# Low parts of the down-projection weights made by VectorE instead of GpSimd in the two feed-forward layers of a hybrid decoder step

## What is computed

```python
def conv_ffn(h, prev, w_up, conv_w, conv_b, w_down):
    u = h @ w_up                                     # 1024 -> 2 * 2816
    t = u.shape[1]
    xp = jnp.concatenate([prev.astype(u.dtype), u], axis=1)
    c = conv_b
    for j in range(CONV_W):
        c = c + conv_w[j] * xp[:, j:j + t]
    val, gate = c[..., :D_FF], c[..., D_FF:]
    return (jax.nn.silu(gate) * val) @ w_down, xp[:, t:]
```

## Time and profile before

| | |
|---|---|
| time, median of 3 runs | 3090.78 us (3090.75 to 3100.58) |
| span of the profiled execution, first to last instruction | 3083.6 us |
| TensorE busy | 2933.5 us (95%) |
| VectorE busy | 1911.6 us (62%) |
| ScalarE busy | 968.2 us (31%) |
| GpSimd busy | 371.0 us (12%) |
| DMA | 174.37 MB, mean 57 GB/s |

### The profile page before, as it was taken

How to read it: one execution, slowest core, us unless ns; L and a number is a source line. 1 busy time by engine, 2 the same in 40 slices (tenths; PEclk the granted TensorE clock), 3 DMA queues, 4 the chain that set the end, 5 groups by cost and what they waited for, 6 DMA issues and landing times. The chain is left out here.

```text
span 3083.6 us, 54554 instructions
## 1 busy us (share of the span) xinstructions
PE 2933.5 (95%) x19232; PEld 2750.7 (89%) x19232; DVE 1911.6 (62%) x3783; ACT 968.2 (31%) x1739; POOL 371.0 (12%) x396
## 2 busy tenths in 40 slices
PE   8979889999998999999999988989989999999998
PEld 5646679998996899999999988989989999999998
DVE  3436667777775565666666666882246566666665
ACT  3433345555554322222222223222122222222221
POOL 1003300000000000000000018660000000000000
PEclk9988999999998999999999999999999999999999
DMA  3010013222221021111111114343111111111111
GB/s 111 28 23 1 35 46 81 73 75 70 75 74 47 27 62 42 41 48 47 48 41 54 35 45 138 87 110 119 49 58 49 42 44 51 41 47 46 49 35 69
DMA packets 262263, 174.37 MB, mean 57 GB/s; under 512 B 77977, under 2 KB 247658, under 8 KB 261818
## 3 DMA queue, kind: packets, MB, share of 16 engines
q1 hardware_dynamic: 261882, 171.85, 19.2%
q10 hardware_dynamic: 192, 0.13, 0.0%
HBM read 149.49 MB, written 22.29 MB: 56 GB/s over the span
## 5 line engine op out<-in xcount | busy, mean ns | idle before, releaser
L1641 PE MATMUL f_up<-h_hi,f_wu_hi 128*128 128x352 f32 x2112 | 460.3, 326 | 16.8 <-DVE h_lo L2155 15.1
L1641 PE MATMUL f_up<-h_hi,f_wu_lo 128*128 128x352 f32 x2112 | 457.6, 324 | 0.0
L1641 PE MATMUL f_up<-h_lo,f_wu_hi 128*128 128x352 f32 x2112 | 457.3, 325 | 0.0
L1641 PEld LDWEIGHTS f_up<-h_hi,f_wu_hi 128*128 128x128 f32 x2112 | 361.8, 190 | 18.0 <-issue 15.7
L1641 PEld LDWEIGHTS f_up<-h_hi,f_wu_lo 128*128 128x128 f32 x2112 | 365.0, 189 | 0.0
L1641 PEld LDWEIGHTS f_up<-h_lo,f_wu_hi 128*128 128x128 f32 x2112 | 361.0, 189 | 0.0
L2068 ACT ACTIVATE f_conv<-f_u_row,f_taps 128x1056 f32<-128x1056 f32 x88 | 111.8, 1271 | 754.1 <-DVE f_u_row L2185 754.1
L2254 DVE TENSOR_TENSOR resid<-resid,f_down 128x352 f32<-128x352 f32 x528 | 271.3, 518 | 111.6 <-PE f_down L2014 108.4
L2014 PE MATMUL f_down<-f_a_hi,f_wd_hi 128*128 (+1 forms) x960 | 318.7, 332 | 6.2 <-DVE resid L2254 5.9
L2014 PE MATMUL f_down<-f_a_hi,f_wd_lo 128*128 (+1 forms) x960 | 311.0, 324 | 0.0
L2014 PE MATMUL f_down<-f_a_lo,f_wd_hi 128*128 (+1 forms) x960 | 310.7, 324 | 0.0
(11 more groups left out here) (428 smaller groups left out, 5678.8 us busy)
## 6 DMA issues: line engine op xcount, KB each, us to landing
f_wu<-ffn_w_up SPq DMA_DIRECT2D x86, 512.0 KB, 3.8
ca_cache<-cache_ckv SPq DMA_DIRECT2D x256, 128.0 KB, 2.0
raw<-ffn_w_down SPq DMA_DIRECT2D x44, 512.0 KB, 4.4
raw<-ssm_w_out SPq DMA_DIRECT2D x16, 512.0 KB, 3.8
s_spill<-resid SPq DMA_DIRECT2D x8, 528.0 KB, 10.5
s_u<-sm_ut SPq DMA_DIRECT2D x8, 528.0 KB, 2.7
resid<-s_spill SPq DMA_DIRECT2D x8, 528.0 KB, 7.9
pj_xb<-x_prompt SPq DMA_DIRECT2D x8, 512.0 KB, 3.7
```

What stands on the lines that cost most here:

```text
L1641: mm = nc.tensor.matmul(out(c), w, x(c), start=(first and n == 0), stop=(last and n == 2))
```

## The change

The low parts of the down weights, 22 subtractions of 128 x 1024 in each layer, leave GpSimd's program and enter VectorE's. In pairs 0 to 9 they stand in the second tile: one behind `low_up` of its value half, one behind `low_up` of its gate half. In pair 10 they stand in the table `between`: behind add 10 and behind add 21 of `down_pair(9)`. GpSimd keeps one memset in these layers.

```diff
@@ @block.gpsimd
-            def low_down(g, jj):
-                pool.wait_ge(wd_hi_done, g * GJ + jj + 1)
-                hi, lo = down_weights(g)
-                if lo is not wd_lo:
-                    pool.wait_ge(up_done, 2 * (NT - 1) + jj + 1)
-                nc.gpsimd.tensor_tensor(lo[:, jj, :], wd[:, :], hi[:, jj, :], ALU.subtract).then_inc(wd_lo_done, 1)
-
             nc.gpsimd.memset(u_row[:, :, 0:2], 0.0).then_inc(zeroed, 1)
-
-            def step(g):
-                if not tiles_in(g):
-                    return
-                low_down(g, 0)
-                low_down(g, 1)
-
-            pairs(pool, step)
@@ @block.vector
+            def low_down(g, jj):
+                dve.wait_ge(wd_hi_done, g * GJ + jj + 1)
+                hi, lo = down_weights(g)
+                nc.vector.tensor_tensor(lo[:, jj, :], wd[:, :], hi[:, jj, :], ALU.subtract).then_inc(wd_lo_done, 1)
@@ last_tiles
                 return {1: lambda: near(0), 3: lambda: near(1), 4: near_new, 6: lambda: far(0), 8: lambda: far(1), 9: far_new,
-                        11: lambda: multiply(j, 0), 13: lambda: multiply(j, 1), 16: lambda: low(j, 0), 18: lambda: low(j, 1)}
+                        10: lambda: low_down(g, 0), 11: lambda: multiply(j, 0), 13: lambda: multiply(j, 1), 16: lambda: low(j, 0),
+                        18: lambda: low(j, 1), 21: lambda: low_down(g, 1)}
@@ step, second tile of pairs 0 to 9
                     all_parts(j, 0)
                     if has_next(g, 1):
                         low_up(j + 1, 0)
+                    low_down(g, 0)
                     all_parts(j, 1)
                     if has_next(g, 1):
                         low_up(j + 1, 1)
+                    low_down(g, 1)
                     for part in (multiply, low):
```

## The result

| | before | after |
|---|---|---|
| time, median of 16 runs | 3093.78 us (3090.24 to 4129.77) | 3087.17 us (3075.95 to 3092.12) |
| ratio after to before | | 0.9978 (95% interval 0.9967 to 0.9988) |
| span of the profiled execution | 3083.6 us | 3087.6 us |
| VectorE busy | 1911.6 us | 1871.4 us |
| GpSimd busy | 371.0 us | 266.9 us |

The change makes the kernel 0.22% faster; I had forecast 0.28%, 3082.2 us. The time lies 0.7 us outside my range of 3078.5 to 3086.5. The kernel before, timed beside the changed one, was itself 3 us slower than the median of 3 runs that I had started from. And the profiled execution after is 4 us longer than the one before, though the kernel is faster: one profile of each does not give this result.

A forecast was written before the change was run, and what follows sets the result against it. TensorE was taken to bound the kernel, with gain only in each layer's last pair: 4.8 us removed less 0.5 added, 4.3 per layer, 8.6 for two, from 3090.8 to 3082.2 us; 8-in-10 range 3078.5 to 3086.5.

The forecast's parts named there:

- TensorE bounds the loop, so the moved subtractions are worth 0 there: Loop over the pairs: TensorE is busy throughout, so moving work between other engines gains 0.
- The holds are GpSimd's subtraction, and go: VectorE's long instructions: held during GpSimd's subtraction, 1.94 us twice per pair in the loop; last pair's TensorE waits 1.01, 1.92.
- In the last pair 4.4 to 5.0 us removed and 0.5 added, 4.3 us per layer: Last pair's down projection: 4.8 us taken for waits and half clock removed, 0.5 added by the subtraction behind add 10.
- the 0.33 us more: Last pair's two holds by the skill page's exclusion rule: 0.33 us more per layer, 3081.5 us in all; not adopted.
- The stretch at half clock ... 1.4 us: Last pair, behind the 1.92 us wait: 11 matmul steps took 3.22 us instead of 1.79; removal gains 1.4 us.
- A further 2 us either way I allow for half-clock stretches of the S5 layer: S5 layer and layer starts: half-clock stretches may shift with the earlier start, each costing up to 1.7 us.
- The level, 3090.8 us: Whole kernel: time before the change from which the forecast gain of 8.6 us was subtracted.
- Since the median lies 7.2 us above that span: Whole kernel: profiled span forecast to fall from 3083.6 to 3075.0 us, with 7.2 us added to get the time.
- Rival A: Last pair: clock falls behind the new 0.5 us wait, 1.4 us less gain per layer, 3085.0 us; chance 0.10.
- B: Last pair: something else holds VectorE, waits stay, subtractions add 0.5 us per layer, 3091.8 us; chance 0.06.
- C: Loop: second block's load starts 1.6 us later; a slow one makes VectorE and TensorE wait, 3106 us; chance 0.04.
- D: Down projections inside the loop: VectorE's freed 1.5 us per pair also removes small waits, 3077 us; chance 0.05.

The follow-up runs named there:

- last_pair_only: Changed kernel with the subtractions of pairs 0 to 9 given back to GpSimd, only the last pair's two on VectorE; ratio to the kernel before 0.9982.
- loop_only: Changed kernel with the last pair's two subtractions given back to GpSimd, those of pairs 0 to 9 on VectorE; 3098.86 us, 1.0029 of the kernel before.
- pool_reads: Changed kernel plus GpSimd subtractions of two SBUF tiles in the last pair, for which nothing waits; 3089.16 us, ratio to the kernel before 0.9992.
- early: Changed kernel with the last pair's first subtraction moved from behind add 10 to VectorE's idle time before the gate half's copy, ScalarE's high part earlier; 3085.86 us.

## Why the prediction was right and wrong

- *TensorE bounds the loop, so the moved subtractions are worth 0 there*: right by the lengths of the feed-forward layers (`last_pair_only`, `loop_only`).
- *The holds are GpSimd's subtraction, and go*: right, and shown by `pool_reads`. They are 1.94 us in the loop and 1.5 and 2.2 us in the last pair. I had expected both savings of a pair in the loop to meet at one copy out of PSUM, whose idle time would grow from 1.81 us to some 3.3. Instead the first shows ahead of the gate half's copy of the same tile (1.94 us before, 2.75 after) and only the second at the place that I had named (2.74 us). That changed nothing in the time.
- *In the last pair 4.4 to 5.0 us removed and 0.5 added, 4.3 us per layer*: right for the first layer. `early`, in which the added 0.5 is gone, lies 4.8 us below the kernel before, which is the 4.8 that I took for the removal; with the whole change it is 4.2 to 4.4 us. The last pair's down projection took 24.6 us where I had named 24.3, and the wait behind add 10 was 0.25 us where I had named about 0.5. My choice of TensorE's waits over the 0.33 us more held as well.
- *"The stretch at half clock ... 1.4 us"* was counted as certain in the second layer, from one execution. Of six profiles with the old last pair and its GpSimd subtractions, it was there in two (`before`, `loop_only`; FF2 790.6 and 790.3 us) and missing in four (787.7 to 788.2). The gain of the second layer was 5.6 us in the first pair of profiles and 2 to 3 us where the stretch was missing. By the mean of six profiles of each kind the two layers gain 4.4 and 3.3 us, 7.7 together, against my 8.6. The timed sets, with 7.8 and 9.0 us, tell neither from the other.
- *"A further 2 us either way I allow for half-clock stretches of the S5 layer"*: this is the step that failed. I priced such a stretch at 3.4 us, 1.7 us of time. In the kernels without extra matmuls the S5 layer took 430.5 to 444.3 us, single stretches lasted up to 23.9 us, and the time at half clock in the layer went from 25.9 to 58.2 us. The stages ahead of the first feed-forward layer add 8 us of their own.
- *The level, 3090.8 us*: it failed by the same omission. It was the median of 3 runs of a kernel whose runs scatter by over 20 us; beside the changed kernel the one before had 3093.78 us. Of the 5.0 us by which 3087.17 missed 3082.2, this is 3.0; the other 2.0 are the gain, 6.6 us by the medians where I had 8.6. Why the level moves by up to 5 us between sets is open. On which side of the bound of 3086.5 the result fell was thus partly chance: the second set of the same kernel, 3080.10 us, lies inside the range.
- *"Since the median lies 7.2 us above that span"*: taken for a fixed distance. Only 1.8 us of it lie around the span; the other 5.4 showed that the profiled execution was one of the shortest, and that was visible before the change ran.
- *Rival A, the half clock behind the small new wait*: did not occur; the wait was 0.25 to 0.28 us in every profile with the subtraction behind add 10, and no fall followed. *B* fell with VectorE's durations. *C*: no wait of VectorE for ScalarE's high part in the trace. *D*: `last_pair_only` shows no gain of the loop.

The change came out within 0.3%, as the likeliest case had it, and its mechanism is the forecast's. The range was too narrow because it was made of the change's terms and not of the kernel's own variation.

## What to carry to other kernels

Ask whether a helper engine's work holds the one whose adds TensorE waits for: here GpSimd's "free" subtraction cost VectorE 1.5 to 2.2 us, more than VectorE's own 1.2, and mattered only in the one place without slack. When a gain of 0.3% is forecast, take the level from many runs and the range from their scatter. Before trusting a profile's level, compare its span with the timed runs: a gap of several us says that the profiled execution is not the usual one. And a stage in which TensorE waits and then makes short matmuls may stay at half clock far longer than the wait; filling the wait with useless matmuls was worth 12 to 14 us, more than the change.

## What the runs showed of the hardware

- A wait of 1.9 us of TensorE was followed by a half-clock stretch of 3.4 us in some executions and by none in others of the same program (FF2 790.6 and 787.8 us): with the old last pair in six of six profiles in the first layer, in two of six in the second.
- A fall of the clock ahead of short matmuls lasted 6.8 us in one execution and 23.9 us in another, though TensorE was busy for 22.8 us of the latter.
- 128x1024 subtracted by GpSimd in 2.4 us held each of VectorE's instructions with two SBUF inputs that it met, by 1.5 to 2.2 us, and once a copy of 128x2 with a single one, by 2.2 us. It held no add with one input in PSUM. 128x2048 written by GpSimd in 1.8 us held none of the four with two SBUF inputs that began beside it.
